# A one-layer hybrid block on one core: segments of 1, 1, 2, 2, 2 tiles instead of 1, 2, 2, 2, 1, two places for weight pieces instead of three, and eleven for gathered rows instead of ten

## What is computed

```
h = rmsnorm(x, norm_mix);  proj = h @ w_in          # q,k,v,r,a of GLA; q,k,v of SWA
y_gla = gla_branch(...) @ w_gla_out                 # gated linear attention, chunks of 64
y_swa = swa_branch(...) @ w_swa_out                 # window attention, 16 heads, sinks, ALiBi
x = x + (sigmoid(gates)[0] * y_gla + sigmoid(gates)[1] * y_swa) @ w_out
# PEER: 8 heads, top 16 of 128x128 product keys, so 128 expert rows for each token
h = rmsnorm(x, norm_ffn);  q = h @ w_q;  scores = q . sub_keys;  top 16 -> eidx, gates
act = gelu(einsum('td,thkd->thk', h, u_tab[eidx]))
x = x + einsum('thk,thkd->td', gates * act, v_tab[eidx])
x = x + sigmoid(rmsnorm(x, norm_ple) @ w_ple_gate) * (p @ w_ple_proj)
return rmsnorm(x, norm_final)
```

## Time and profile before

| what | value |
|---|---|
| median of 3 runs | 3558.37 us (3557.22 to 3565.75) |
| the profiled execution, its own time | 3558.73 us |
| its span | 3556.9 us |
| granted TensorE clock over the span | 0.907 |
| busy: PE, PE weight load, DVE, ACT, POOL | 81%, 54%, 71%, 40%, 36% |
| moved by DMA | 1376.58 MB, mean 387 GB/s |
| of it gathered rows / the SyncE queue | 1073.81 MB / 300.51 MB |

### The profile page before, as it was taken

The page is one execution under the profiler, slowest core; times in us unless marked ns, Lnnn a source line. Parts: engine busy times, 40 slices in busy tenths (PEclk is TensorE's granted clock), DMA queues, the critical chain, the costliest instruction groups (busy, mean ns, idle before and its releaser), DMA issues.

```text
span 3556.9 us, 35414 instructions
## 1 busy us (share of the span) xinstructions
PE 2871.3 (81%) x11192; PEld 1930.2 (54%) x11192; DVE 2532.2 (71%) x5329; ACT 1419.6 (40%) x3606; POOL 1284.6 (36%) x1028
## 2 busy tenths in 40 slices
PE   8878978899878787686998889778878687686765
PEld 7767856776544455363665557454445355363323
DVE  0248877767888887699678876798566756677664
ACT  2333453324344443334344453434343443433522
POOL 0014332323454444344434433433334333344441
PEclk9989989999989899888999899889999899898987
DMA  6589988989999999999999999999999999999995
GB/s 237 172 320 421 377 315 327 365 331 384 421 422 415 404 421 421 420 392 404 422 421 420 405 383 412 416 413 395 422 421 421 421 410 421 420 417 412 421 421 218
DMA packets 195916, 1376.58 MB, mean 387 GB/s; under 512 B 22401, under 2 KB 24321, under 8 KB 32018
## 3 DMA queue, kind: packets, MB, share of 16 engines
q0 software_dynamic: 147456, 1073.81, 73.5%
q1 hardware_dynamic: 48274, 300.51, 21.4%
HBM read 1363.22 MB, written 11.01 MB: 386 GB/s over the span
## 4 chain that ended last, share of the span: by engine, by line
PE 34%; DMA 30%; DVE 18%; issue 9%; ACT 7%; POOL 2%; another core or an unknown queue 0%; DVEq 0%; POOLq 0%; ACTq 0%; SPq 0%
DMA uv<-in_uv,idx 29%; PE bank L588 13%; PE ysum L780 8%; PE bank L598 8%; DVE acc L1321 5%; DVE uv L1293 4%; POOL uv L545 2%; PE bank L657 2%; DVE lidx L1146 1%; DVE vals L1143 1%; ACT bufX L856 1%; DMA slab<-in_slabs 1%; DVE bufE L1140 1%; DVE bufX L1111 1%; ACT bufX L813 1%
## 5 line engine op out<-in xcount | busy, mean ns | idle before, releaser
L545 POOL DMA_INDIRECT uv<-in_uv,idx x1024 | 1284.4, 1254 | 2214.9 <-DVE acc L1321 1033.5
L1293 DVE SCALAR_TENSOR_TENSOR uv<-uv,hbuf 128x1024 f32<-128x1024 f32 x1024 | 1247.2, 1223 | 550.8 <-DMA uv<-in_uv,idx 526.4
L780 PE MATMUL ysum<-uv,diag 128*128 128x512 f32 x2152 | 1121.3, 665 | 418.7 <-ACT diag L1044 416.4
L780 PEld LDWEIGHTS ysum<-uv,diag 128*128 128x128 f32 x2152 | 433.6, 211 | 965.9 <-ACT diag L1044 514.1
L1321 DVE SCALAR_TENSOR_TENSOR acc<-uv,dots,acc 128x1024 f32<-128x1024 f32 x486 | 622.3, 1281 | 86.6 <-ACT dots L1035 69.9
L1030 ACT ACTIVATE dots<-dots 128x2 f32<-128x2 f32 x512 | 103.0, 201 | 1148.3 <-DVE uv L1293 1137.0
L588 PE MATMUL bank<-bufA,slab 128*128 128x256 f32 (+1 forms) x2400 | 439.3, 342 | 5.5 <-ACT bufB L813 5.4
L588 PEld LDWEIGHTS bank<-bufA,slab 128*128 128x128 f32 x2400 | 390.8, 194 | 74.1 <-issue 36.4
L598 PE MATMUL bank<-slab,bufA 128*128 128x256 f32 x1408 | 318.1, 385 | 4.9 <-ACT bufA L842 3.7
L598 PEld LDWEIGHTS bank<-slab,bufA 128*128 128x128 f32 x1408 | 271.3, 194 | 63.5 <-issue 20.8
L1035 ACT ACTIVATE dots<-dots,gexp 128x1 f32<-128x1 f32 x1024 | 245.9, 287 | 20.9 <-ACT dots L1030 0.4
(11 more groups left out here) (146 smaller groups left out, 2426.5 us busy)
## 6 DMA issues: line engine op xcount, KB each, us to landing
slab<-in_slabs SPq DMA_DIRECT2D x255, 1024.0 KB
uv<-in_uv,idx POOLq DMA_INDIRECT x1024
x_d<-acc SPq DMA_DIRECT2D x7, 512.0 KB, 8.1
bufA<-in_x SPq DMA_DIRECT2D x3, 1024.0 KB
bufA<-x_d SPq DMA_DIRECT2D x3, 1024.0 KB
out<-bufA SPq DMA_DIRECT2D x3, 1024.0 KB
bufE<-in_g_ffn SPq DMA_DIRECT2D x5, 512.0 KB, 9.0
bufX<-in_g_fin SPq DMA_DIRECT2D x5, 512.0 KB, 20.9
```

The source lines that it names most:

```text
L545: nc.gpsimd.indirect_dma_start(out=uv[:, at % NS, :], out_offset=None, in_=a["uv"], in_offset=bass.IndirectOffsetOnAxis(ap=idx[:, g % 4, k ...
L780: ins = mm(ysum[:, c, :], diag[:, m % DS, :], uv[:, at % NS, D + c * 512:D + c * 512 + 512], start=(m == first), stop=(m == last))
L1293: v.scalar_tensor_tensor(out=row, in0=row, scalar=1.0, in1=hbuf[:, i % HB, :], op0=ALU.mult, op1=ALU.mult, accum_out=dots[:, g % 3, k:k + ...
```

## The change

The segments become 1, 1, 2, 2, 2 tiles. The due step of segment 1 is 28 (before 50), and those of segments 2, 3, 4 are 114, 242, 370 (before 178, 306, 434). The closing of segment 0 goes two items a step. Tail groups 0 and 1 are hosted by segments 3 and 4; group 2 now stands alone. `slab` has 2 places, `uv` 11. Tiles 0 and 1 give every third row to TensorE from their seventh row on, so that TensorE adds 38 rows of tile 0 (before 21), 38 of tile 1 (before 61), 61 of tile 5 (before 92), and 501 in all (before 538). The lists `vals` and `lidx` of the first top-k get three places, used in turn.

```
-SEGS = (1, 2, 2, 2, 1)
+SEGS = (1, 1, 2, 2, 2)
...
-RS = 3
+RS = 2
...
-NS = 10
+NS = 11
 HB = 2
+
+LS = 3
...
 ODD = tuple(range(1, TOPK, 2))
+SOME = tuple(range(1, TOPK, 3))
 MOST = tuple(k for k in range(TOPK) if k % 4)
-ON_PE = [MOST, ODD, ODD, ODD, ODD, MOST, MOST, MOST]
-
-SPARE = [100] + [6] * (NTILE - 1)
-IS_PE = [at % TOPK in ON_PE[at // (NH * TOPK)] and at % (NH * TOPK) >= SPARE[at // (NH * TOPK)] and at < ROWS - 4
+ON_PE = [SOME, SOME, ODD, ODD, ODD, ODD, MOST, MOST]
+
+SPARE = 6
+IS_PE = [at % TOPK in ON_PE[at // (NH * TOPK)] and at % (NH * TOPK) >= SPARE and at < ROWS - 4
          for at in range(ROWS)]
...
-HOST = {0: 2, 1: 3, 2: 4}
+HOST = {0: 3, 1: 4}
...
+DUE = [AT_ONCE - 2, PER_TILE // 2 - 4] + [PER_TILE * AT[s] - AHEAD - 2 for s in range(2, NSEG)]
...
-        due = PER_TILE * AT[s] - AHEAD - 2 if s else AT_ONCE - 2
+        due = DUE[s]
         last = len(names) - 1
         begin = found[-1][0] + 1 if found else due - last
         for i, n in enumerate(names):
             stand(s, n, begin + i * (due - begin) // last)
-        more, gap = closing(s), 2 if s in GUEST else 1
-        for i, (of, n) in enumerate(more):
-            stand(of, n, due + gap * (i + 1))
+        pace = 2 if s in GUEST else 1 if s else 0.5
+        for i, (of, n) in enumerate(closing(s)):
+            stand(of, n, due + math.ceil(pace * (i + 1)))
...
-        vals = sb("vals", [P, TT, NH, 2, TOPK])
-        lidx = sb("lidx", [P, TT, NH, 2, TOPK], U32)
+        vals = sb("vals", [P, LS, NH, 2, TOPK])
+        lidx = sb("lidx", [P, LS, NH, 2, TOPK], U32)
```

More of the change, by code:

```diff
@@ L1 @@
+import math
 from contextlib import ExitStack
@@ L1134, in largest @@
                     for half in range(2):
-                        lists.append((vals[:, t, h, half, :], lidx[:, t, h, half, :],
+                        slot = (AT[s] + t) % LS
+                        lists.append((vals[:, slot, h, half, :], lidx[:, slot, h, half, :],
                                       ysc[:, h % 2, t, half * NK:half * NK + NK]))
@@ L1222, in topk @@
                 i, h = divmod(m, NH)
-                slot = i - AT[seg_of(i)]
+                slot = i % LS
                 val = vals[:, slot, h]
```

## The result

The changed kernel took 3601.51 us (median of 4 runs, 3597.65 to 3610.51), the kernel before 3558.36 us. The ratio is 1.0117, with a 95% interval of 1.0099 to 1.0136. The forecast was 3536 us with a range from 3485 to 3590, so the time lies outside it, on the side of the rival in which the loads become the wait.

The account below looks back on a forecast made before the run. Tile 0 was taken as bound by TensorE's work, and the kernel from about step 80 on by bytes. Terms: 272 + 930 + 2290 + 42 = 3534 us of span, with 1.8 us more 3536 us; range 3485 to 3590.

Parts of the forecast that it names:

- the rival in which the loads become the wait: Steps 0 to 27, TensorE at each piece's start: 46 us more at an 11 us load, 3582 us; chance 23%.
- steps 128 to 511: Late, byte-bound stretch: 25 pieces fewer save 62 us, 3 us more gain left; 2290 us.
- Head: Up to the first dot: 10 us for two-place loads and 14 us for stages put ahead, first dot at 272 us.
- Steps 0 to 27: Early tile 0: 37 pieces at 6.0 us are 224 us, plus 11 us for a chain of loads; 235 us.
- TensorE's 39 us of attention: Steps 0 to 27: attention of one tile and subkeys, some 39 us of TensorE's 205 us sum.
- Steps 28 to 127: Rest of tile 0: steps 28 to 49 bound by bytes, 165 us; steps 50 to 127, 530 us (500 to 560).
- The 7% of friction: Steps 50 to 127: DMA time lost with VectorE and TensorE both near 92% busy, giving 530 us from 497 of bytes.
- Tile 5's rows: Tile 5: 31 rows moved from TensorE to VectorE, 40 us of VectorE's time, taken as hidden.
- The slower rival: Steps 0 to 27: TensorE waits for piece loads; decides from 3569 us, at a load of 10.3 us; chance 23%.
- The sign named for it: Sign of a wrong forecast: TensorE's waits for slab over 60 us in all, or in the two-tile fronts.
- The full-DMA rival: Steps 0 to 27 and 50 to 127: DMA stays at 421 GB/s with 7.0 us loads; 3491 us, chance 17%.

Follow-up runs that it names:

- half pieces: Changed kernel with each piece load after the first places bringing half its bytes: 3479.6 us; same with three piece and ten row places: 3437.3 us.

## Why the prediction was wrong

**What bounds.** Tile 0 bound by TensorE, the rest by bytes: the direction held. The new order alone is faster (20 us), and steps 128 to 511 came 5 us from the forecast. That is partly luck: with three and ten places they took 2304 us, 51 us under before instead of the 65 forecast; of the other 19 us, 10 came with giving up the third place for pieces (2294) and 9 with the eleventh for rows (2285). And with half pieces those steps gave back only about half of the bytes' time, so bytes alone do not set it.

**Head: right sum, wrong terms.** The forecast was 10 us for the loads and 14 us for the stages put ahead of the first dot. The runs give 21 us (old order) to 26 us (new order) for the places, and nothing for the stages: the first dot is at 247 to 248 us in both orders with three places. The ten pairs were counted rightly for the old order (ten waits; thirteen in the new), but a wait is 1.5 us, not 1.0, mostly since the quiet load is 4.9 us and not 4.5; and 5 us of slower work of TensorE were not in the sum. The stages' 14 us never came.

**Steps 0 to 27: the step that failed.** The forecast took the largest of three sums: bytes 204 us, TensorE 205, pieces 37 x 6.0 = 224, and added 11. So it let everything but the pieces (attention, subkeys, rows) disappear behind the loads. The load was sized right (8.5 us; 8.4 on average); the overlap was wrong. The stretch falls into three parts:

```profile
274.00:393.00 119.00, 91.36 (x505) 74.47 (x505) 69.22 (x151) 42.76 (x94) 25.08 (x20) 0.94 0.91 355
393.00:470.00 77.00, 61.31 (x363) 44.96 (x364) 52.18 (x99) 41.53 (x102) 17.72 (x16) 0.87 0.81 322
470.00:569.00 99.00, 65.75 (x376) 55.75 (x374) 44.55 (x79) 31.14 (x68) 23.77 (x17) 0.87 0.88 344
```

In the first, 18 pieces were asked for, 6.6 us each, and TensorE waited 27 us for pieces; in the third 14 pieces, 7.1 us each, and 26 us. Here (load + use) / 2 is near, with a few rows on top. Between them stands the window attention: 7 pieces in 77 us, and 1 us of waits for them. Its work more than covered the loads of its own seven pieces and none of the others. Work stands at fixed points of TensorE's program and hides a load only if it stands between that load's request and its use, so a largest-of-sums for the whole stretch was too low, by 60 us. With three places the same account is 212 us of work, 20.5 of waits for pieces and 23 for VectorE's stages, close to the 259 us measured. So the exchange cost 36 us there, where the forecast had it at about 20 us over the bytes; and three places, too, leave loads in the open at this density.

A smaller slip: TensorE's 39 us of attention was 203 less 46 pieces, but only 43 of segment 0's pieces stand ahead of the first dot. With 43 it is 50 us, and TensorE's sum 216 instead of 205, against 218 measured.

**Steps 28 to 127.** 152 us against 165, and 546 against 530, inside its bounds. TensorE's waits for pieces in the second are 13.0 us on L597, in two-tile stages where the forecast had none. They are not the price of the second place: with three places they are 12.0 us and the stretch 537 us. The 7% of friction was right by luck (497 us of bytes at 389 instead of 421 GB/s is 8%): by the rates in the earlier trace rows, 361, 328 and 345 GB/s, tile 0's windows had lost 14 to 22%, not 7 to 22.

**The table of rows.** Tile 5's rows were costed at nothing; the table is worth 27 us, 17 of them in tile 5. The reason given, that VectorE had room there, was right; what was overlooked is that TensorE had little (385 of 428 us busy with the old table).

**The slower rival.** Its place was right and so was its wait. Its price formula, 37 x (load - 8.5) / 2, gives 0 to 11 us at the loads measured (8.4 on average, 9.1 as median), and the 33 us that it needed called for 10.3 us. It had the same fault as the forecast: what failed was not the length of the load but what covers it. Its chance of 23% was too low for that reason. The sign named for it, over 60 us of waits for pieces in all, came true with 103.7.

**The full-DMA rival** rested on a load of 7 us. The rule of the Trainium skill behind it (DMA: Bandwidth & Descriptors, Queues, rings and completion order) is that each DMA engine takes turns between its queues packet by packet. A load of 7 us is not borne out: 8.4 us on average, and the stretch's rate was 343 GB/s. How a load shortens fits the rule better. Half pieces have as many packets, each half as large, so by turns a load loses only its own bytes' time, 0.52 MB at 421 GB/s or 1.25 us (an estimate); the trace has 1.5 us. The turns themselves are not shown.

## What to carry to other kernels

A ring of places is a length of time: with n places a load has n - 1 uses, and what stands between them, to land in, and it has to be held against the load's time *with the other queues busy*, read from the trace of a small transfer in the same stretch. An in-order engine's work hides a load only if it stands between that load's request and its use; elsewhere work and wait add. So cut a stretch into runs of loads and runs of other work and add these up, instead of taking the largest of sums over the whole. When a change trades one buffer for another and moves work as well, run the places and the order as a two-by-two before believing either: here the order was worth -20 us with three places and +9 us with two.

## What was not expected of the hardware

While 1 MB gathers ran, a load of 0.5 MB in as many packets was only 1.5 us shorter than one of 1 MB (6.9 against 8.4 us on average), and without gathers 1.3 us (3.6 against 4.9 as median). In the head that was enough to take away most of the wait (first dot at 256 us against 274, three places 247 to 249). And the price of a place for gathered rows is uneven: ten to eleven gave 11 to 13 us, nine to ten 31 us, though the DMA share already read 0.99 to 1.00 in the late stretches with ten.
